# Norm entries of a two-block transformer kernel begun inside the program that feeds them, GpSimd making each entry's first low halves, and an opening that waits for less

## What is computed

```python
for l in range(DEPTH):                       # 2
    h = rms_norm(x, attn_norm[l])
    proj = h @ w_in[l]                       # attention, difference attention, gated scan
    x = x + mix @ w_out[l]
    hf = rms_norm(x, ffn_norm[l]) @ w_up[l]
    gate, val = hf[..., :D_FF], hf[..., D_FF:]
    gate = depthwise_conv(gate, conv_w[l], conv_b[l])
    x = x + (gelu(gate) * val) @ w_down[l]
```

```python
    h = layer_norm(ALPHA * x + mix @ w_out[l], ln1_g[l], ln1_b[l])
    x = layer_norm(ALPHA * h + peer_ffn(h, ...), ln2_g[l], ln2_b[l])
```

## Time and profile before

| | us |
|---|---|
| median of 3 runs (2822.35 to 2829.43) | 2827.97 |
| profiled execution, its own time | 2826.24 |
| span of its instructions | 2824.5 |
| PE busy in the span | 2651.6 (94%) |
| DVE busy | 2054.0 (73%) |
| ACT busy | 1496.3 (53%) |
| GpSimd (POOL) busy | 176.2 (6%) |
| mean granted PE clock | 0.979 |

### The profile page before, as it was taken

The page is one execution under the profiler, slowest core; times in us unless marked ns, Lnnn a source line. Parts: engine busy times, 40 slices in busy tenths (PEclk is TensorE's granted clock), DMA queues, the critical chain, the costliest instruction groups (busy, mean ns, idle before and its releaser), DMA issues. The chain is left out here.

```text
span 2824.5 us, 56598 instructions
## 1 busy us (share of the span) xinstructions
PE 2651.6 (94%) x17272; PEld 2387.2 (85%) x17272; DVE 2054.0 (73%) x4610; ACT 1496.3 (53%) x2949; POOL 176.2 (6%) x136
## 2 busy tenths in 40 slices
PE   7989999989988899799999999988998999999997
PEld 6869988779977899799988888777998999888886
DVE  5767767767767668877767777787589777677777
ACT  5545556645555444466655555555454566555554
POOL 0000000000000044300000000000344000000000
PEclk9989999989999999999999999999999999999999
DMA  5225654236653477555567777625576555677775
GB/s 194 86 68 166 186 154 162 74 112 184 186 162 101 150 222 225 165 171 176 174 199 233 234 233 232 213 92 174 174 230 192 160 175 171 187 233 235 232 234 179
DMA packets 194306, 503.49 MB, mean 178 GB/s; under 512 B 22561, under 2 KB 88353, under 8 KB 192801
## 3 DMA queue, kind: packets, MB, share of 16 engines
q1 hardware_dynamic: 194208, 502.28, 56.8%
HBM read 467.59 MB, written 34.60 MB: 178 GB/s over the span
## 5 line engine op out<-in xcount | busy, mean ns | idle before, releaser
L182 DVE TENSOR_TENSOR w_lo<-w_raw,w_hi 128x512 fp32r<-128x512 f32 (+1 forms) x1464 | 994.8, 684 | 357.3 <-ACT w_hi L173 337.4
L173 ACT ACTIVATE w_hi<-w_raw 128x512 fp32r<-128x512 f32 (+2 forms) x1592 | 925.7, 621 | 203.4 <-PE banks_right L217 136.7
L215 PE MATMUL up_up<-hT_hi,w_hi 128*128 128x256 f32 x2048 | 595.8, 291 | 26.6 <-DVE w_lo L182 20.5
L217 PE MATMUL up_up<-hT_hi,w_lo 128*128 128x256 f32 x2048 | 582.6, 284 | 0.0
L216 PE MATMUL up_up<-hT_lo,w_hi 128*128 128x256 f32 x2048 | 582.3, 284 | 0.0
L215 PEld LDWEIGHTS up_up<-hT_hi,w_hi 128*128 128x128 f32 x2048 | 396.1, 193 | 31.2 <-DVE w_lo L182 23.9
L227 PE MATMUL banks_left<-w_hi,expert_hi 128*128 128x512 f32 x1024 | 408.1, 399 | 7.8 <-DVE w_lo L182 7.8
L228 PE MATMUL banks_left<-w_lo,expert_hi 128*128 128x512 f32 x1024 | 407.6, 398 | 0.0
L229 PE MATMUL banks_left<-w_hi,expert_lo 128*128 128x512 f32 x1024 | 407.4, 398 | 0.0
L216 PEld LDWEIGHTS up_up<-hT_lo,w_hi 128*128 128x128 f32 x2048 | 395.6, 193 | 0.0
L217 PEld LDWEIGHTS up_up<-hT_hi,w_lo 128*128 128x128 f32 x2048 | 395.0, 193 | 0.0
(11 more groups left out here) (374 smaller groups left out, 3863.6 us busy)
## 6 DMA issues: line engine op xcount, KB each, us to landing
w_raw<-in_peer_u_c SPq DMA_DIRECT2D x256, 512.0 KB, 3.5
w_raw<-in_peer_v SPq DMA_DIRECT2D x256, 512.0 KB, 3.6
w_raw<-in_w_up_c SPq DMA_DIRECT2D x88, 512.0 KB, 3.7
expert_gelu_held<-expert_gelu SPq DMA_DIRECT2D x256, 128.0 KB, 1.7
expert_back<-expert_gelu_held SPq DMA_DIRECT2D x256, 128.0 KB, 3.3
w_raw<-in_w_down SPq DMA_DIRECT2D x44, 512.0 KB, 4.1
w_raw<-in_w_in_r SPq DMA_DIRECT2D x40, 512.0 KB, 3.6
w_raw<-in_w_in_c SPq DMA_DIRECT2D x32, 512.0 KB, 4.0
```

Of the source, the lines that this page charges most:

```text
L173: self.nc.scalar.activation(self.w_hi[:, k % SLOTS, 0:width], self.raw_half(k, width), ACT.Copy).then_inc(self.sem("w_hi_done"), 1)
L182: self.nc.vector.tensor_tensor(self.w_lo[:, k % SLOTS, 0:width], self.raw_half(k, width), self.w_hi[:, k % SLOTS, 0:width].bitcast(F32), A ...
L215: self.nc.tensor.matmul(bank, hi, self.hT_hi[:, c, :], start=(c == 0), stop=False)
L217: last = self.nc.tensor.matmul(bank, lo, self.hT_hi[:, c, :], start=False, stop=(c == DC - 1))
```

## The change

Four things change.

First, the block that feeds an entry computes its last products a token tile at a time (`last_halves`; the last output chunk in the first mixer and the feed-forward, the last two in the second mixer and the down phase). While PE still works on tile 1, DVE adds tile 0's two column halves and half 0 of tile 1 (`early_vector`), ACT makes the next entry's first two `w_hi` and, for an RMS norm, tile 0's squares (`early_scalar`); for a layer norm, DVE makes tile 0's statistics and inverse, and ACT loads the root's table and takes the root.

Second, behind the barrier tile 1 of an RMS entry is scaled by ACT and DVE, a half each, and turned by plain transposes; only tile 0 goes through the scaled identity. A layer-norm entry normalises both tiles in place and uses plain transposes for both. The high and low chunks are released to PE one at a time in places.

Third, GpSimd makes an entry's first four `w_lo` (`split_lo_too`), which DVE made before; the next low on DVE waits for them. In `finish`, GpSimd multiplies tile 0 by the gain and adds the bias, DVE does tile 1, and the output leaves in four transfers.

Fourth, the opening waits for `x` (two transfers), the identity and `cols1` alone; `cols2` and `iota` count on another semaphore, waited for at the end of the first mixer's SP queue.

```diff
+    def last_halves(self, pe, chunks, acc, done):
+        for t in range(TT):
+            cols = slice(t * P, (t + 1) * P)
+            for i, (k, act_hi, act_lo) in enumerate(chunks):
+                end = i == len(chunks) - 1
+                for h in range(2):
+                    if t == 0:
+                        pe.wait_ge(self.sem("w_lo_done"), k + h + 1)
+                    hi, lo = self.w_hi[:, (k + h) % SLOTS, :], self.w_lo[:, (k + h) % SLOTS, :]
+                    bank = acc[:, t, h, :]
+                    self.nc.tensor.matmul(bank, act_hi[:, cols], hi, start=False, stop=False)
+                    self.nc.tensor.matmul(bank, act_hi[:, cols], lo, start=False, stop=False)
+                    last = self.nc.tensor.matmul(bank, act_lo[:, cols], hi, start=False, stop=end)
+                    if t == TT - 1:
+                        last.then_inc(self.sem("w_used"), 1)
+                    elif end:
+                        last.then_inc(done, 1)
...
+    def arrived(self, dve, t, h):
+        if t == 0:
+            dve.wait_ge(self.acc_done, h + 1)
+        else:
+            dve.wait_ge(self.K.sem("w_used"), self.k0 - 1 + h)
+    def add_half(self, t, h):
+        x = self.x[:, t, h]
+        return self.K.nc.vector.tensor_tensor(x, x, self.add[:, t, h], ALU.add)
+    def early_vector(self, dve):
+        for t, h in ((0, 0), (0, 1), (1, 0)):
+            self.arrived(dve, t, h)
+            self.add_half(t, h).then_inc(self.added, 1)
+    def early_scalar(self, act, junk=None):
+        for h in range(2):
+            self.K.split_hi(act, self.k0 + h, self.width)
...
+    def pool(self, pool):
+        for h in range(EARLY):
+            self.K.split_lo_too(pool, self.k0 + h, self.width)
...
+    def square(self, act, t, h, junk):
+        if self.add is not None:
+            act.wait_ge(self.added, 2 * t + h + 1)
+        self.K.nc.scalar.activation(junk, self.x[:, t, h], ACT.Square,
+                                    accum_out=self.K.ns[:, t, h:h + 1]).then_inc(self.squared, 1)
+    def sqrt(self, act, t):
+        act.wait_ge(self.squared, 2 * t + 2)
+        act.wait_ge(self.based, t + 1)
+        ns = self.K.ns[:, t]
+        self.K.nc.scalar.activation(ns[:, 3:4], ns[:, 1:2], ACT.Sqrt, scale=1.0 / D, bias=ns[:, 2:3]).then_inc(self.root, 1)
+    def base(self, dve, t):
+        dve.wait_ge(self.squared, 2 * t + 1)
+        ns = self.K.ns[:, t]
+        self.K.nc.vector.tensor_scalar(ns[:, 2:3], ns[:, 0:1], 1.0 / D, EPS1, ALU.mult, ALU.add).then_inc(self.based, 1)
+    def early_scalar(self, act, junk):
+        super().early_scalar(act)
+        for h in range(2):
+            self.square(act, 0, h, junk[:, h])
+    def tensor(self, pe):
+        pe.wait_ge(self.scaled, 1)
+        for c in range(DC):
+            self.K.nc.tensor.matmul(self.ps[:, c, 0:P], self.K.x[:, 0, c * P:(c + 1) * P], self.diag[:], start=True, stop=True)
+        for c in range(DC):
+            if c == 0:
+                pe.wait_ge(self.left_half, 1)
+            if c == DC // 2:
+                pe.wait_ge(self.right_half, 1)
+            self.turn(c, 1, self.rows)
+    def scalar(self, act):
+        K, A = self.K, self.K.nc.scalar
+        if self.add is None:
+            self.early_scalar(act, self.spare[:, 0])
+        self.sqrt(act, 0)
+        for h in range(2):
+            self.square(act, 1, h, self.spare[:, 0, h])
+        self.sqrt(act, 1)
+        act.wait_ge(self.scaled, 2)
+        A.activation(self.spare[:, 1, 0], self.x[:, 1, 0], ACT.Copy, scale=K.ns[:, 1, 4:5]).then_inc(self.left_half, 1)
+        K.split_hi(act, self.k0 + 2)
+        for j in range(DC // 2):
+            act.wait_ge(self.turned, j + 1)
+            for c in (2 * j, 2 * j + 1):
+                A.activation(K.hT_hi[:, c, :], self.ps[:, c, :], ACT.Copy, scale=self.gain[:, c:c + 1]).then_inc(self.hi_done, 1)
+            if j == 1:
+                K.split_hi(act, self.k0 + 3)
+    def vector(self, dve):
+        K, V = self.K, self.K.nc.vector
+        link = lambda ins: K.dve.link(dve, ins)
+        self.base(dve, 0)
+        if self.add is not None:
+            self.add_half(1, 1).then_inc(self.added, 1)
+        dve.wait_ge(self.root, 1)
+        link(V.reciprocal(K.ns[:, 0, 4:5], K.ns[:, 0, 3:4]))
+        V.tensor_scalar(self.diag[:], K.ident[:], K.ns[:, 0, 4:5], None, ALU.mult).then_inc(self.scaled, 1)
+        self.base(dve, 1)
+        dve.wait_ge(self.root, 2)
+        V.reciprocal(K.ns[:, 1, 4:5], K.ns[:, 1, 3:4]).then_inc(self.scaled, 1)
+        dve.wait_ge(self.scaled, 2)
+        V.tensor_scalar(self.spare[:, 1, 1], self.x[:, 1, 1], K.ns[:, 1, 4:5], None, ALU.mult).then_inc(self.right_half, 1)
+        for j in range(DC // 2):
+            dve.wait_ge(self.hi_done, 2 * j + 2)
+            for c in (2 * j, 2 * j + 1):
+                V.scalar_tensor_tensor(K.hT_lo[:, c, :], self.ps[:, c, :], self.gain[:, c:c + 1],
+                                       K.hT_hi[:, c, :].bitcast(F32), ALU.mult, ALU.subtract).then_inc(self.lo_done, 1)
...
+    def add_half(self, t, h):
+        x = self.x[:, t, h]
+        return self.K.nc.vector.scalar_tensor_tensor(x, x, ALPHA, self.add[:, t, h], ALU.mult, ALU.add)
...
+    def inverse(self, dve, t):
+        dve.wait_ge(self.root, t + 1)
+        V, ns = self.K.nc.vector, self.K.ns[:, t]
+        self.K.dve.link(dve, V.reciprocal(ns[:, 3:4], ns[:, 2:3]))
+        V.scalar_tensor_tensor(ns[:, 4:5], ns[:, 0:1], -1.0, ns[:, 3:4], ALU.mult, ALU.mult).then_inc(self.ready, 1)
+    def norm_act(self, act, t, part):
+        act.wait_ge(self.ready, t + 1)
+        x, ns = self.K.x[:, t, part], self.K.ns[:, t]
+        self.K.nc.scalar.activation(x, x, ACT.Identity, scale=ns[:, 3:4], bias=ns[:, 4:5]).then_inc(self.rows_act, 1)
+    def early_vector(self, dve):
+        link = lambda ins: self.K.dve.link(dve, ins)
+        for h in range(2):
+            self.arrived(dve, 0, h)
+            link(self.add_half(0, h))
+            ins = self.stats(0, h)
+        link(ins)
+        self.variance(dve, 0)
+        self.arrived(dve, 1, 0)
+        link(self.add_half(1, 0))
+        self.K.dve.mark(self.stats(1, 0))
+        self.inverse(dve, 0)
+    def early_scalar(self, act, junk=None):
+        if self.gain is not None:
+            super().early_scalar(act)
+        self.K.nc.scalar.activation(self.K.ns[:, 0, 5:6], self.K.eps[:, 1:2], ACT.Sqrt)
+        self.sqrt(act, 0)
+    def last_stats(self, dve):
+        link = lambda ins: self.K.dve.link(dve, ins)
+        link(self.add_half(1, 1))
+        link(self.stats(1, 1))
+        self.variance(dve, 1)
...
+    def tensor(self, pe):
+        for t in range(TT):
+            for c in range(DC):
+                if c == 0:
+                    pe.wait_ge(self.rows_act, t + 1)
+                if t == 1 and c == DC // 2:
+                    pe.wait_ge(self.rows_dve, 1)
+                self.turn(c, t, self.K.x[:, t])
+    def scalar(self, act):
+        K, A = self.K, self.K.nc.scalar
+        self.norm_act(act, 0, slice(0, D))
+        self.sqrt(act, 1)
+        self.norm_act(act, 1, slice(0, D // 2))
...
+        def low(c, n):
+            dve.wait_ge(self.hi_done, c + n)
+            part = slice(c, c + n)
+            V.tensor_tensor(K.hT_lo[:, part, :], self.h[:, part, :], K.hT_hi[:, part, :].bitcast(F32),
+                            ALU.subtract).then_inc(self.lo_done, n)
+        shift(1)
+        low(0, 1)
+        low(1, 1)
+        low(2, 2)
+        shift(3)
+        low(4, 2)
+        low(6, 2)
...
-            down_tile(LAST, 0, at(LAST))
+            pe.wait_ge(lo_done, LAST + 1)
+            K.last_halves(pe, [(at(LAST), ac_hi[:, LAST % 2, :], ac_lo[:, LAST % 2, :])], acc, following.acc_done)
...
+        self.following.early_vector(dve)
 
     def tensor_tile(self, pe, j, n):
+        last = isinstance(n, int) and n == self.ROUNDS - 1 and j >= BODY - 2
+        if last:
+            if j == BODY - 1:
+                first = self.k0 + 2 * SLOTS * n
+                pe.wait_ge(self.lo_done, NK)
+                self.K.last_halves(pe, [(first + 2 * i, self.hi[:, i % 2, :], self.lo[:, i % 2, :]) for i in (BODY - 2, BODY - 1)],
+                                   self.acc, self.following.acc_done)
+            return
         pe.wait_ge(self.lo_done, j + 1 + BODY * n)
-        last = isinstance(n, int) and n == self.ROUNDS - 1 and j == BODY - 1
         for h in range(2):
             self.K.out_half(pe, self.k0 + 2 * j + h, self.hi[:, j % 2, :], self.lo[:, j % 2, :], self.acc, h,
-                            start=(is_first(n) and j == 0), stop=last, rep=n)
+                            start=(is_first(n) and j == 0), stop=False, rep=n)
...
+            @block.gpsimd
+            def _(pool):
+                pool.wait_ge(norm.rows_act, 1)
+                pool.wait_ge(*rows_in)
+                for h in range(2):
+                    nc.gpsimd.tensor_tensor(x[:, 0, h], x[:, 0, h], gain[:, h], ALU.mult).then_inc(scaled, 1)
```

(21 more changed lines are left out.)

393 lines of the change are left out of this document (176 added, 217 removed).

## The result

The changed kernel takes **2781.9 us** (median of 4, 2780.3 to 2786.8) against 2827.6 of the kernel before (median of 4): ratio 0.9844, 95% interval 0.9827 to 0.9862. In the profiled executions the span went from 2824.5 to 2780.1.

The account below looks back on a forecast made before the run. TensorE was taken as busy inside feed-forward loops, with time lost between blocks. Terms 2 x 2.9 + 3.0 + 2.0 + 5.2 + 2.2 + 5.3 + 0 = 23.5 us gave 2804.5 us at the median; range 2797 to 2815.

Parts of the forecast that it names:

- more overlaps than I count: Rival 3: finish +2.3, no lock in the layer norms +1.3, opening +1, giving 2799 us; chance 0.12.
- Opening 5.3: Opening, to the first tile's end: start no longer waits for `iota`, then the weights' landing sets it; gain 5.3 us.
- First mixers 2.9 each: First mixer to feed-forward, twice: sums and squares made early, tile's end at 213.8 instead of 216.7; gain 2.9 us each.
- Second layer's mixer 3.0: Feed-forward to second layer's mixer: 3.6 us shorter despite a bare table load, 3.0 counted because PE may lose its clock.
- rival 2: The clock stays low: after the new gaps it falls on real products, 1 to 2 us over six entries; 2812, chance 0.13.
- Third mixer 2.0: Feed-forward to third mixer: tile 0's sums leave the path, first product 2.95 us after the start instead of 5.0; gain 2.0.
- Query projections 2.6 each: Second mixer to query projection, twice: start 1.4 us late, tile's end 929.3 instead of 931.9; gain 2.5 and 2.6.
- Fourth mixer 2.2: Down phase to fourth mixer: start 2.8 us late, entry 5.9 shorter to its first product, net 2.6; 2.2 counted.
- GpSimd's lows free: Entries' first four lows on GpSimd: 1.3 us each, nothing waits; 0.45 charged per layer-norm DVE low for the lock.
- Finish 0: Finish: late start, shorter work, GpSimd's and DVE's operations one after the other; gain 0, bounds -1.0 and +2.3.
- Rival 1: DVE's scalings queue behind GpSimd: PE 0.3 to 1.6 us late in three RMS entries, up to 5.8; 2810, chance 0.15.
- Rival 4: Early part prolongs the feeding block: nine places at 3.8 us more each give 2835, slower; chance 0.02.

Follow-up runs that it names:

- a_pad96: The changed kernel with 96 more unused bytes per partition behind the two new norm buffers, so the expert phases' tiles lie as before the change: 2803.1 us.
- a_warm: The changed kernel with idle transposes of the identity on TensorE in the waits of its RMS and layer-norm entries: 2777.6 us.
- a_dve_lows: The changed kernel with the entries' first four lows back on the vector engine, GpSimd doing none of them: 2783.9 us.

## Why the prediction was wrong

The step that failed is the first. "What bounds the kernel" has it that a feed-forward loop is "185.5 of 188.0 us" busy, so that "work off PE is hidden there, and what costs time lies between blocks". A busy TensorE was taken for one whose pace is given, and the sum put the bodies at nothing. TensorE's pace depends on where tiles lie in SBUF, and the change moved them by two small buffers: the bodies gave 21.7 of the 44.4 us, 21.0 of them in the expert phases. No rival named it either; the nearest, *more overlaps than I count*, put the missing time in the entries. With the old placement (a_pad96) the same change measures 2803.1 against the 2804.5 forecast.

The sum over the entries, 22.7 for 23.5, is closer than its terms, and part of that is luck: the query projections and the second layer's mixer gave 4.1 us less than forecast, the first mixers, the fourth mixer and the finish 3.5 more. All three signs of being wrong that the prediction names came true in part: scalar rows of DVE stretched, the granted clock was 0.50 under first tiles, and the first tile's end moved less than its first product.

Point by point:

- *Opening 5.3*: 5.0. The weights' landing sets it as said (9.24 for 9.1).
- *First mixers 2.9 each*: 3.4 and 3.3. Start, scaled identity and first product came as said or 0.5 earlier.
- *Second layer's mixer 3.0*: 1.6. Here rival 2 came true: the table load leaves TensorE idle for 3.2 us, the clock is 0.50 from 397.58 to 403.33, and the turns take 5.7 us. In a_pad96, where the clock was 1.00 there, and in a_warm, the gain is 3.4.
- *Third mixer 2.0*: 2.1. The parts listed add up to 3.3 us, not 2.95, which would be a gain of 1.7; the first product comes 3.2 us behind the last one.
- *Query projections 2.6 each*: 1.2 and 1.3. The first product did come 4.2 us earlier (7.9 us behind the last one, 12.1 before), the start was 1.1 later behind it (forecast 1.4), and then the tile took 6.9 us instead of 3.9. Of the miss of 1.4 the clock explains all in the first projection (13.3 in a_warm, 13.1 forecast); the charge of 0.45 for GpSimd's lock is 0.5 in a_dve_lows.
- *Fourth mixer 2.2*: 4.1 in this profile, 1.9 in a_pad96, where the low clock lay on the tile (mean 0.65), so 4.1 is the lucky end. The prediction's own figures, 5.9 less 2.8, are 3.1 and not its 2.6. The wait for the last expert tile is 1.13, as said; the start comes 1.6 behind the last product, for 1.5.
- *GpSimd's lows free*: yes (a_dve_lows).
- *Finish 0*: 0.7. GpSimd's and DVE's operations hold each other up, as the timeline shows. DVE's take 1.3 to 1.8 us each, for the 0.67 forecast without the lock. The eight take 6.8 us from the first start to the last end, where strictly one behind another was to be 7.9:

```profile
2768.49 1.26 POOL L3158 TENSOR_TENSOR x<-x,w_raw 128x512 f32<-128x512 f32 x1 [610.16 <-ACT x L496]
2768.97 3.00 DVE L3174 SCALAR_TENSOR_TENSOR x<-x,norm_scalars,w_raw 128x512 f32<-128x512 f32 x2
2769.83 1.59 POOL L3160 TENSOR_TENSOR x<-x,w_raw 128x512 f32<-128x512 f32 x1
2771.38 1.70 POOL L3158 TENSOR_TENSOR x<-x,w_raw 128x512 f32<-128x512 f32 x1
...
2772.08 3.23 DVE L3178 SCALAR_TENSOR_TENSOR x<-x,norm_scalars,w_raw 128x512 f32<-128x512 f32 x2
2773.16 1.59 POOL L3160 TENSOR_TENSOR x<-x,w_raw 128x512 f32<-128x512 f32 x1
```

Rival 1, DVE's scalings behind GpSimd, came true at the low end of its price. In the two entries behind a first mixer the scaling of the identity (`norm_scale`) begins 0.8 us into a low of GpSimd and takes 0.55 us, and that of tile 1's half 0.62. First the changed kernel, then a_dve_lows, whose GpSimd makes no lows:

```profile
198.41 2.62 POOL L200 TENSOR_TENSOR w_lo<-w_raw,w_hi 128x512 fp32r<-128x512 f32 x2 [175.96 <-POOLq L981]
199.22 0.55 DVE L442 TENSOR_SCALAR norm_scale<-ident,norm_scalars 128x128 f32<-128x128 f32 x1
200.69 0.62 DVE L447 TENSOR_SCALAR ffn_spare<-x,norm_scalars 128x512 f32<-128x512 f32 x1
```

```profile
197.00 0.29 DVE L446 TENSOR_SCALAR norm_scale<-ident,norm_scalars 128x128 f32<-128x128 f32 x1
198.80 0.49 DVE L452 TENSOR_SCALAR ffn_spare<-x,norm_scalars 128x512 f32<-128x512 f32 x1
```

So TensorE's turn, which waits for the scaled identity, starts 0.26 us late in two of the three RMS entries. In the third, the second layer's mixer, the scaling meets only the last 0.2 us of a low and keeps its length:

```profile
394.84 2.60 POOL L200 TENSOR_TENSOR w_lo<-w_raw,w_hi 128x512 fp32r<-128x512 f32 x2 [189.20 <-POOLq L707]
...
397.23 0.30 DVE L442 TENSOR_SCALAR norm_scale<-ident,norm_scalars 128x128 f32<-128x128 f32 x1
```

In all three the scaling ends 0.08 or 0.09 us behind the low that it met. The rule for `tensor_scalar` of the Trainium skill, page "SBUF — State Buffer", section "Who interferes with whom", is that in a two-port mode the later of the two waits, and the traces agree with it. The first mixers gained more than forecast in spite of it.

Rival 2 came true where the low clock fell on first tiles, at 1.5 and 1.8 us in two entries by a_warm. Rival 4, the longer feeding block, holds only by its counted parts; its "2835" is not what nine places at 3.8 us make (2804.5 + 34.2 = 2838.7).

What stays open: why the distance between tiles changes TensorE's pace and which accesses meet; whether tiles that TensorE doesn't read have any part in it; why the up step has two paces at one distance; and whether distances that no run tried do better still.

## What to carry to other kernels

Before you forecast a change, list which tiles it moves: a few bytes allocated early shift everything behind them, and in a loop where TensorE is always busy that can weigh as much as the change. Compare the mean distance between product starts before and after, loop by loop, not the busy share; and try two or three paddings of the operands' tiles against each other, for here the best gave 31.5 us on top of the change. Count distances by the full address: two places that look alike modulo 128 had different paces here. A step begun in the feeding program gains by being early, not by being cut smaller; but a shorter wait followed by work at the low clock returns part of it.

## What the runs showed of the hardware

- The step between 128x512 fp32r products was 226.7, 228.9, 232.4, 233.3 or 234.3 ns, with the placement of tiles alone, at a granted clock of 1.00: at distances of 0, 192, 128, 32, 64 or 224, and 96 bytes modulo 256 from `w_hi` to `expert_hi`. Between 128x256 products the means were 116.0 to 119.9, the lowest with a distance of 64 from `hT_hi` to `w_hi`, where single stretches ran at 113.2 or 117.8.
- The spread between executions of one kernel (2780.3 to 2786.8) is of the size of what the clock does in the mixers: the fourth mixer's body was 108.6 us in the profile of before and 114.7 in that of the changed kernel, 109.1 in a_pad96, with one, three and two stretches at the low clock in it.
- DVE's subtraction of two SBUF tiles of 512 columns took 1.35 us beside GpSimd and 0.68 without. Its scaling by a per-partition column took 0.55 and 0.29 for 128 columns, 0.62 and 0.49 for 512; it took 0.30 where GpSimd's operation had 0.2 us left.
